# A two-layer mLSTM and windowed-attention trunk on one core: the token-wise input projection in column groups of 264, 512 and 512, and a first mLSTM chunk that starts without a barrier

## What is computed

```python
h = _rmsnorm(x, norm1_g[l])
z = h @ w_in[l]
mq, mk, mv, mi, mf, mo, aq, ak, av = jnp.split(z, split_idx, axis=-1)
qk = jax.nn.silu(_causal_dwconv(jnp.concatenate([mq, mk], axis=-1), conv_w[l], conv_b[l]))
hm = _mlstm_chunkwise(mq, mk, mv, i_pre, f_pre)          # 4 heads of 128, a recurrence over chunks
hm = _rmsnorm(hm, mlstm_norm_g[l]) * jax.nn.sigmoid(mo)
ha = _swa_sinks(aq, ak, av, sinks[l])                    # 8 query heads, 2 key heads of 64
x = x + jnp.concatenate([hm, ha], axis=-1) @ w_out[l]
h2 = _rmsnorm(x, norm2_g[l])
x = x + jnp.square(jax.nn.relu(h2 @ w_ff1[l])) @ w_ff2[l]
```

## Time and profile before

| | us |
|---|---|
| median of three runs | 2230.84 |
| the profiled execution | 2231.89 |
| its span in the trace | 2230.0 |
| PE busy | 2140.7 (96%) |
| POOL busy | 988.0 (44%) |
| DVE busy | 1424.1 (64%) |
| ACT busy | 857.6 (38%) |

### The profile page before, as it was taken

How to read it: one execution, slowest core, us unless ns; L and a number is a source line. 1 busy time by engine, 2 the same in 40 slices (tenths; PEclk the granted TensorE clock), 3 DMA queues, 4 the chain that set the end, 5 groups by cost and what they waited for, 6 DMA issues and landing times.

```text
span 2230.0 us, 34286 instructions
## 1 busy us (share of the span) xinstructions
PE 2140.7 (96%) x11748; PEld 1805.8 (81%) x11748; DVE 1424.1 (64%) x1674; ACT 857.6 (38%) x1459; POOL 988.0 (44%) x697
## 2 busy tenths in 40 slices
PE   6999998989999999999999999899899999999998
PEld 6998877878788877888899887788878887778886
DVE  4127865467777777676640488654677777876764
ACT  4224333345666642121231343432556666321210
POOL 3334524324555555445522455143245555454542
PEclk9999999999999999999999999899999999999999
DMA  7322225415777788776532223254166677987663
GB/s 261 105 92 76 72 94 179 136 70 168 255 254 241 239 304 314 306 281 256 215 129 86 90 77 111 83 174 151 39 209 237 237 237 249 348 313 292 270 273 142
DMA packets 227662, 427.29 MB, mean 192 GB/s; under 512 B 24936, under 2 KB 167016, under 8 KB 219248
## 3 DMA queue, kind: packets, MB, share of 16 engines
q1 hardware_dynamic: 212336, 402.93, 51.0%
q10 hardware_dynamic: 15232, 23.16, 2.9%
HBM read 272.79 MB, written 157.43 MB: 193 GB/s over the span
## 4 chain that ended last, share of the span: by engine, by line
PE 58%; issue 19%; POOL 12%; DVE 5%; ACT 2%; SPq 1%; DMA 1%; ACTq 1%; POOLq 0%; DVEq 0%
PE ps L1368 23%; PE ps L1714 20%; POOL w1s L1309 8%; PE ps L1553 7%; POOL w2s L1313 3%; PE ps L1666 1%; DMA uk<-uD 1%; PE ps L1472 1%; DVE y L1756 1%; DVE hT L1762 1%; PE ps L1499 1%; PE ps L1486 1%; PE ps L1591 1%; PE ps L1592 1%; PE ps L1359 1%
## 5 line engine op out<-in xcount | busy, mean ns | idle before, releaser
L1714 PE MATMUL ps<-w2s,uk 128*128 128x512 f32 x2688 | 618.6, 392 | 7.6 <-DVE uf L2249 4.1
L1714 PEld LDWEIGHTS ps<-w2s,uk 128*128 128x128 f32 x2688 | 504.8, 189 | 120.2 <-issue 11.4
L2213 DVE TENSOR_TENSOR xs<-ps,xs 128x1024 f32<-128x1024 f32 x208 | 253.4, 1222 | 171.6 <-PE ps L1714 169.9
L1666 PE MATMUL ps<-hT,w1s 128*128 128x512 f32 x1344 | 317.8, 392 | 10.6 <-DVE uf L2175 4.7
L1666 PEld LDWEIGHTS ps<-hT,w1s 128*128 128x128 f32 x1344 | 250.1, 188 | 73.4 <-issue 12.5
L1313 POOL TENSOR_TENSOR w2s<-raw,w2s 128x1024 fp32r<-128x1024 f32 x64 | 182.0, 2866 | 181.3 <-ACT w2s L1088 181.3
L1309 POOL TENSOR_TENSOR w1s<-rawf,w1s 128x512 fp32r<-128x512 f32 x112 | 170.2, 1531 | 194.3 <-ACT w1s L982 194.3
L1368 PE MATMUL ps<-hT,whi 128*128 128x512 f32 x768 | 246.3, 402 | 0.0
L1368 PE MATMUL ps<-whi,hT 128*128 128x258 f32 x1280 | 238.2, 286 | 1.0 <-DVE hT L1762 0.6
L1666 PE MATMUL ps<-tT,w1s 128*128 128x512 f32 x1008 | 237.3, 389 | 0.0
L1666 PEld LDWEIGHTS ps<-tT,w1s 128*128 128x128 f32 x1008 | 189.1, 188 | 39.5
(11 more groups left out here) (209 smaller groups left out, 3318.7 us busy)
## 6 DMA issues: line engine op xcount, KB each, us to landing
uk<-uD SPq DMA_DIRECT2D x64, 1024.0 KB, 8.7
raw<-in_wstream SPq DMA_DIRECT2D x104, 512.0 KB, 5.6
uk<-uD SPq DMA_DIRECT2D x64, 768.0 KB, 7.8
rawf<-in_wstream SPq DMA_DIRECT2D x64, 512.0 KB, 4.3
uD<-uh SPq DMA_DIRECT2D x64, 512.0 KB, 5.1
uD<-uf SPq DMA_DIRECT2D x64, 512.0 KB, 5.3
uD<-uh SPq DMA_DIRECT2D x64, 384.0 KB, 4.1
uD<-uf SPq DMA_DIRECT2D x64, 384.0 KB, 5.0
```

Of the source, the lines that this page charges most:

```text
L1666: mm = pe.matmul(ps[:, bank, :], w, x[:, k, :], start=(first and k == 0 and i == 0), stop=(k == 3 and i == 2), skip_group_check=True)
L1714: mm = pe.matmul(ps[:, bank + tp, :], u, w2s[r][:, w, k, :], start=(r in (1, 2, 5) and k == 0 and i == 0), stop=(k == 1 and i == 2), skip_ ...
L2213: V.tensor_tensor(y, ps[:, bank:bank + 2, :], y, ALU.add).then_inc(y_acc, 1)
```

## The change

Stage A has three groups of 264, 512 and 512 columns, so 24 tiles in place of 40. The arrays that the host lays out are the same, so a unit is now put together from pieces: two transfers each for units 0 to 5, three each for units 6 to 9. Group 2's split weights lie over `xs` (ACT waits for the store of x ahead of group 1). ACT splits units 2 to 5 during group 0, units 6 to 9 during group 1, and does the exponentials and squares within group 2. Group 0's result is stored by two transfers a tile.

Barrier 2 is gone (`PHASES` is 2). In the last step of stage B PE does chunk 0's scores and keys inside the last `big`, DVE's `first_chunk` weights them there, ACT and POOL split the first attention tile there. In stage C PE takes `w_out` row by row (`row`, `out_split`): rows 0 to 3 in chunk 0 and rows 4 to 7 in chunk 1, each as soon as it is split, both column halves at once. The attention half of `mxh` is multiplied with these rows first. POOL splits the `lo` of k = 3, 4 and 6, DVE of 0, 1, 2, 5 and 7. Chunk 0 doesn't multiply with the state, which is zero there.

The ring is 4 x 4 x 264 x 4 = 16896 bytes, 33 x 512, and `whi` and `wlo` are `D` words long: in the changed kernel `whi`, `wlo`, `mxh`, `mxl`, `ahi1`, `alo1`, `ahi2`, `alo2` leave 224 when divided by 512, as `hT` does.

```diff
+GC = (264, 512, 512)
+ZX = ZV + 512 - 6
...
-        raw = [ring_r(f"raw{s}", [P, 4 * GW], F32) for s in range(RING)]
+        raw = [ring_r(f"raw{s}", [P, 4 * GC[0]], F32) for s in range(RING)]
         hilo_at = ring_r.at
-        whi = [ring_r(f"whi{s}", [P, 4 * GW], F32R) for s in range(RING)]
-        wlo = [ring_r(f"wlo{s}", [P, 4 * GW], F32R) for s in range(RING)]
+
+        ahi0, alo0 = [ring_r(f"a{n}0", [P, KT, GC[0]], F32R) for n in ("hi", "lo")]
+        ahi1_at = ring_r.at
+        ahi1 = ring_r("ahi1", [P, KT, 512], F32R)
+        br = Region(hilo_at)
+        whi = [br(f"whi{s}", [P, D], F32R) for s in range(RING)]
+        br = Region(ahi1_at)
+        wlo = [br(f"wlo{s}", [P, D], F32R) for s in range(RING)]
...
                 sp.wait_ge(w_lo, l * U + max(n + 1, RING))
-                sp.dma_start(raw[slot][:], wtoken[l, n]).then_inc(s_raw[slot], 16)
+
+                def piece(g, kh, k0, ks, c0, dst):
+
+                    src = wtoken[l, 2 * g + kh].rearrange("p (k c) -> p k c", c=GW)
+                    sp.dma_start(dst, src[:, k0:k0 + ks, c0:c0 + dst.shape[2]]).then_inc(s_raw[slot], 16)
+
+                if n < 2:
+                    d = raw[slot][:].rearrange("p (k c) -> p k c", c=GC[0])
+                    piece(0, n, 0, 4, 0, d[:, :, 0:GW])
+                    piece(4, n, 0, 4, ZX - 4 * GW, d[:, :, GW:GC[0]])
+                else:
...
+                    if n < 6:
+                        piece(1, kh, k0, 2, 0, d[:, :, 0:GW])
+                        piece(2, kh, k0, 2, 0, d[:, :, GW:512])
...
-                barrier(sp, p_sp, (p_pe, p_act, p_dve, p_pool), l * PHASES + 2)
...
-                    if t in (2, 3):
-                        split_a(l, t, 0, 0)
+                    if 2 <= t < 6:
+                        if t == 2 and l > 0:
+
+                            act.wait_ge(y_m, l * YM)
+                        split_a(l, t)
...
+                act.wait_ge(n_y, (l * 2 + 1) * NT)
+                act.wait_ge(s_spill, l * (32 * NT) + 16 * NT)
+                for t in range(NT):
+                    if t < 4:
+                        split_a(l, 6 + t)
+                    evacuate(1, t)
+                for t in range(NT):
+                    evacuate(2, t)
...
-                att_hi(0, 0)
-                for k in range(4):
-                    split_out(k)
+                split_out(0); split_out(1)
                 squares(0, 0)
+                split_out(2)
                 decays(0, 1, False)
+                split_out(3)
...
+                        for k in range(KT):
+                            if last and x == 5 and k == 5:
+
+                                pe.wait_ge(b_at, (l + 1) * NT + 1)
+                                pe.wait_ge(b_pd, (l + 1) * NT + 1)
+                                scores_c(0, 0, 0, l * NT)
+                                keys_t()
...
+                    if first:
+
+                        pe.wait_ge(c_al, T + 1)
+                        pe.wait_ge(c_x, T * 2 + 2)
+                        for k in range(4):
+                            out_split(pe, l, k)
+                            for n in range(2):
+                                row(p, n, ROW[k])
...
+                def first_chunk():
+                    dve.wait_ge(c_rin[0], l * 64 + 16)
+                    V.tensor_copy(scl[:].unsqueeze(2), erB[0][:, :, P - 1:P]).then_inc(c_scl, 1)
+                    weights(0, l * NT, False)
```

More of the change, by code:

```diff
@@ L104, in trunk_kernel @@
         ta = Region(tmp_at)
-        zst = [ta(f"zst{b}", [P, GW], F32) for b in range(4)]
+        zst = [ta(f"zst{b}", [P, 512], F32) for b in range(4)]
         gN = ta("gN", [P, NT, 8], F32)
@@ L898, in _ @@
                 step_b(MH - 1, True)
-                for b in range(2):
-                    act.wait_ge(b_ao[b], (l + 1) * 64 + 1)
-                barrier(act, p_act, (p_pe, p_sp, p_dve, p_pool), l * PHASES + 2)
                 def split_out(k):
@@ L1299, in _ @@
                 plain_lo(0, 0); plain_lo(0, 1)
-                barrier(pool, p_pool, (p_pe, p_sp, p_dve, p_act), l * PHASES + 3)
-                for _ in range(4):
+                barrier(pool, p_pool, (p_pe, p_sp, p_dve, p_act), l * PHASES + 2)
+                for _ in range(5):
                     pool.sem_inc(w_lo, 1)
@@ L1423, in rows_m, with step_b @@
                     mm.then_inc(a_mn, 1)
-                group(1, 2)
-                rows_b()
-                group(2, 0)
+                for n in range(NT):
+                    tile(1, n)
+                    if n == 3:
+                        rows_b()
                 rows_t()
-                group(3, 2)
-                rows_m()
-                group(4, 0)
+                for n in range(NT):
+                    tile(2, n)
+                    if n == 3:
+                        rows_m()
                 barrier(pe, p_pe, (p_act, p_sp, p_dve, p_pool), l * PHASES + 1)
-                def step_b(j):
+                def step_b(j, last):
                     T = [l * NT + j * 2, l * NT + (j * 2 + 1)]
@@ L1445, in big @@
                         pe.wait_ge(b_ev, H + (x + 1))
-                        mm = three(ps[:, G + x % 2, :],
-                                       [(whi[s][:, k * P:(k + 1) * P], wlo[s][:, k * P:(k + 1) * P], hT[:, x % 2, 0, k, :], hT[:, x % 2, 1, k, :])
-                                        for k in range(KT)])
+                        for k in range(KT):
[4 more added lines that the diff above has]
+                                keys_t()
+                            h_, l_ = whi[s][:, k * P:(k + 1) * P], wlo[s][:, k * P:(k + 1) * P]
+                            for i, (a, b) in enumerate(((h_, 0), (h_, 1), (l_, 0))):
+                                mm = pe.matmul(ps[:, G + x % 2, :], a, hT[:, x % 2, b, k, :], start=(k == 0 and i == 0), stop=(k == KT - 1 and i == 2))
                         mm.then_inc(b_g, 1)
@@ L1529, in keys_t, with row @@
                     mm.then_inc(c_kt, 1)
-                pe.wait_ge(b_at, (l + 1) * NT + 1)
-                pe.wait_ge(b_pd, (l + 1) * NT + 1)
-                scores_c(0, 0, 0, l * NT)
-                keys_t()
-                barrier(pe, p_pe, (p_act, p_sp, p_dve, p_pool), l * PHASES + 2)
+                with pe.Fori(0, MH - 1) as j:
+                    step_b(j, False)
+                step_b(MH - 1, True)
+                def row(p, n, k):
+                    w, m = slice(n * 512, (n + 1) * 512), (k + 4) % KT
+                    for a, b in ((mxh, woh), (mxh, wol), (mxl, woh)):
+                        mm = pe.matmul(ps[:, G + n, :], a[p][:, m, :], b[:, k, w],
+                                       start=(k == 4 and a is mxh and b is woh), stop=(k == 3 and a is mxl), skip_group_check=True)
+                    return mm
                 def project(T, p, n, att_part, mix_part):
@@ L1543, in project @@
                         pe.wait_ge(c_x, T * 2 + (n + 1))
-                    for part, ks in ((att_part, range(4, KT)), (mix_part, range(0, 4))):
-                        if not part:
-                            continue
-                        if ks[0] == 0:
-                            pe.wait_ge(c_mh, T + 1)
-                            pe.wait_ge(c_ml, T + 1)
-                        for k in ks:
-                            w = slice(n * 512, (n + 1) * 512)
-                            for a, b in ((mxh, woh), (mxh, wol), (mxl, woh)):
-                                mm = pe.matmul(ps[:, G + n, :], a[p][:, k, :], b[:, k, w],
-                                               start=(k == 4 and a is mxh and b is woh), stop=(k == 3 and a is mxl))
+                        for k in range(4, KT):
+                            row(p, n, k)
                     if mix_part:
+                        pe.wait_ge(c_mh, T + 1)
+                        pe.wait_ge(c_ml, T + 1)
+                        for k in range(4):
+                            mm = row(p, n, k)
                         mm.then_inc(c_op, 1)
@@ L2042, in step_c @@
                     V.tensor_tensor(mixf[:], ps[:, TB + 1, :].rearrange("p (h c) -> p h c", c=P), gst[p][:], ALU.mult).then_inc(c_mix, 1)
-                    if not (first or second):
+                    if second:
+                        residual(l, j, p, 0, 1)
+                    if not first:
                         residual(l, j, p, 1, 1)
```

274 lines of the change are left out of this document (152 added, 122 removed).

## The result

The changed kernel is slower: 2237.97 us (median of nine runs, 2236.91 to 2241.63) against 2230.73 (nine runs of the kernel before, 2227.98 to 2234.17), ratio 1.0033 with a 95% interval of 1.0024 to 1.0042. The forecast was 2214.9, and the range of 2202 to 2229 doesn't hold the result. The profiled execution's span is 2235.3 us against 2230.0.

A forecast was written before the change was run, and what follows sets the result against it. PE, busy 2140.7 of 2230.0 us, was taken as the bound. Terms -14.2, +2, +15, -8.3 and -10.4 sum to -15.9, from 2230.84 to 2214.9 us; range 2202 to 2229.

The forecast's parts named there:

- The weights at the start: Program start: short rows of units 0 and 1 in shared queues delay PE's first stage A product, +15 us.
- R2: Rival, program start: small rows travel in groups, so the start is as early as before; 2199.9 us, chance 0.13.
- Fewer, wider matmuls: Stage A: two groups of 512 columns replace four of 258, and an ACT wait goes; -14.2 us for both layers.
- ACT stall: Last group of stage A: PE idle 1.6 us a layer while ACT does exponentials and squares, claimed to go.
- Group 0: Stage A's first group: six more columns, more DMA issues, splits and subtractions; +2 us for both layers, bounds 0 and 6.
- The distance between matmuls in B and C: Stages B and C: new start addresses of stationary operands bring matmuls 6.0 ns closer; -10.4 us, bounds 0 and -12.
- The entry of stage C: From stage B's end to stage C's even pace: the wait for wd goes, chunk 2 starts earlier; -8.3 us.
- R3: Rival, entry of stage C: gives nothing, since splits, not the barrier, were what C waited for; 2223.2 us, chance 0.09.
- R4: Rival, entry of stage C: PE's clock falls to 1.2 GHz in the first two chunks; slower, 2254.9 us, chance 0.08.

The follow-up runs named there:

- e1: Changed kernel, but the host lays out each stage A weight unit as used, one transfer of 128 rows instead of two or three; 2222.78 us, ratio 0.9969.
- e2: Changed kernel, but SP issues the 8 copies of x to the output behind unit 3, instead of ACT; 2227.43 us, ratio 0.9987.
- e7: e1 with columns in the order of the groups, so group 0's result is stored by one transfer a tile, not two; 2218.30 us, ratio 0.9932.
- e10: Changed kernel, but POOL's mask additions for chunks 0 and 1 wait until PE has transposed the last tile's probabilities; 2233.09 us, ratio 1.0010.
- e6: Changed kernel with the barrier of all five engines between stages B and C put back; 2240.26 us, ratio 1.0037.
- e3: Changed kernel, but DVE, not POOL, splits row 6 of w_out, behind hn of chunk 1; 2234.52 us, ratio 1.0009.
- e8: e3 with DVE also splitting row 4 of w_out, right behind chunk 1's keys; 2232.06 us, ratio 0.9999.
- e9: Kernel before with only addresses changed: whi, mxh, mxl at 224 or 480 past a multiple of 512, stage B's wlo at 256, 320, 352; 2230.01 us, ratio 0.9989.
- e12: e11, but DVE splits row 6 of w_out right behind the state update and ahead of hn, row 7 behind hn; 2201.21 us, ratio 0.9867.
- e11: Changed kernel with e7, e8 and e10 together; 2209.11 us, ratio 0.9896.

## Why the prediction was wrong, by its own steps

*The weights at the start*: right. +15 forecast, +15.3 measured; unit 0 at 28.2 (29.1), `gB` at 29.8 (30.4), unit 1 at 31.9 (33.3), the first product at 37.2 (37). The last link was another one, and that the number is so close is in part luck: I had PE wait for POOL's split of unit 1, which ended at 36.3; it waited for `hT`, ready at 37.2, at the end of the chain that `gB` begins. e1 and e2 gave 21.87 and 25.79 where 22 and 25.5 were forecast from turns of the two queues. R2, by which nothing would be lost there, is out: the Trainium skill's typical 9 to 17 descriptors to a packet (DMA: Bandwidth & Descriptors, Queues, rings and completion order) don't show in these counts, 139 against 138 in the stretch above.

*Fewer, wider matmuls*: -14.2 forecast, -11.1 measured. The matmuls gave what was forecast: without the gates' sums and the barrier, the wide groups of a layer take 93.5 us before and 87.7 after, 5.8 less for the 5.7 forecast. Inside them a tile's 24 starts take 5.44 us (226.7 ns each); the 229.4 of the runs of 96 comes from the first tile behind a row of small matmuls (5.55 to 5.61). The step that failed is the "ACT stall" of 1.6 us a layer. There was none: the 1.64 us in which PE was idle between 126 and 153 us are its wait at barrier 1, at the first matmul of B:

```profile
152.99 0.74 PE L1462 MATMUL ps<-ident,rq 128*128 128x128 f32 x5 [1.56 <-ACTq L354]
```

After the change this wait is 1.77 us. I read an idle share of a stretch whose end lay behind the barrier, and gave the idle time to what ACT was doing in it. A sum over a stretch needs the one row that holds the gap.

*Group 0*: +2 forecast, +5.0 measured, inside the bounds. I counted the eight DMA issues among the things "beside PE's products". In the second layer they are in a chain: copy of the result, store, store, copy of `hT`, DVE, PE. e7 shows that this was the whole of it there.

*The distance between matmuls in B and C*: -10.4 forecast; the cause was right and the size 5 ns rather than 6, which would be 8.6. Measured in B and C are 5.3. In stage B of the first layer 23 products gain 0.12 us each, 2.8 in all, and the layer's B still ends 0.2 later. The gain went into a wait that was there before, 1.43 us for `rq` and now 2.11 (and 0.61 at another step, where there was none), and one product after it ran at 1.2 GHz for part of its time, 7.3 us from first start to last end for 5.7. In the second layer the gain of 3.2 is near the forecast 3.5, because the kernel before had already lost there what the changed one loses: a wait of 2.33 us and a product of 6.7 behind it. I took PE as the bound all through B because it was 96% busy; at the last step of B the bound is DVE's chain to `rq`, and closer matmuls can only wait longer for it. e10 took the wait away, and then they were worth their price: stage B up to its last product takes 164.3 us in the first layer, 168.1 before.

*The entry of stage C*: -8.3 forecast, -1.5 measured; the largest miss, and what R3 had named. The first half was right to 0.1 us: chunk 0's `mixf` came 13.5 us after B's last matmul (forecast 13.4). The second half failed at chunk 1. I had written its chain as 9.4 us from `mixf` and a POOL split behind it. It took 10.7: DVE stood for 2.0 us while POOL split row 4. I had seen this cost (1 us a layer, bounds of 13 us in all) and estimated it away with "most of the chain's DVE steps fall between them". Here the Trainium skill's rule (SBUF — State Buffer, Who interferes with whom) would have done better than my average: DVE and GpSimd hold a common port pair for whole instructions. As the page has it, this holds for a DVE instruction with two inputs in SBUF, beside a GpSimd instruction that reads SBUF, and not for one with at most one such input outside DVE's two-port modes. So "each meeting", as I had put it, was too wide. The rows above agree with both halves: the step at 357.04 reads two SBUF operands and ends at 359.17, POOL's split at 359.15; the copy at 356.84 reads PSUM and takes its 0.16 us. And 1.6 us a layer went to the clock after the 4.18 us wait, where I had argued that the new waits would each be under 2 us. That is R4's mechanism at a tenth of its size: 1.2 GHz came for seven matmuls after a wait, not for two chunks.

*Stage D* wasn't in the sum and cost 2.8. In both layers the fifth run of 24 matmuls in D began after the same 2.06 us wait as before and took 4.62 us in place of 3.14. The change may not be the cause. Behind this wait the same 24 matmuls take 3.13 us in both layers of e6 and in one layer of e3, e7 and e8, with the code of D as it is, and 4.39 in one layer of e9, which is the kernel before at other addresses. Why the clock falls after it in one place and not in the other is open.

Of the 21 us that are missing, the entry of C has 6.8, the distance in B and C 5.1, the wide groups 3.1, group 0 3.0 and stage D 2.8. The range failed because the two largest have a common ground: what PE gains ahead of a place where it waits for another engine's chain is given back there, and behind the wait the clock can take some more. Each of my rivals touched one term and let the others stand in full.

## What to carry to other kernels

Count a transfer in a shared queue by its rows, before its bytes; if the host may lay data out, let it do so in the order and width of use. For each gain on the busiest engine, name the next place where that engine waits, and what the awaited chain is made of: an engine that comes there earlier only waits longer. A POOL instruction beside a DVE chain can cost its own length in that chain (2.0 us at 357 us), and so can a split of DVE's own that stands in the chain, so splits and masks belong where the chain isn't awaited (e10 and e12: some 12 us for two moved steps).

## What was not expected of the hardware

- The start address of a stationary operand changes the distance between matmuls of 512 columns by some 5 ns: 224 and 480 past a multiple of 512 give 5.46 to 5.48 us for 24, and 256, 288 and 352 give 5.57 to 5.61. One of two alternating operands at a slow start brings most of the loss (e9: 5.55). The two fast starts are 256 bytes apart, which suggests that period; which other starts are fast, and why, is open.
- The granted clock falls after some waits of 2 to 4 us and not after others of the same length: in e8 a wait of 3.01 us was followed by twelve matmuls in 5.49 us, one of 3.03 by twelve in 3.03. Behind a wait of 1.73 us for `rq` the product took 5.73 us in the first layers of e6 and e7, and 7.3 in the second layer of e3. What sets it besides the wait is open.
- Outside stage D, matmuls of 512 columns that took 0.6 us or more number 12 before, 30 after the change, 14 in e10, 8 in e12, but 33 in e11, which is 29 us faster than the changed kernel. This isn't a loss of the change as a whole: before it the entry of C ran other, smaller matmuls at 1.2 GHz (granted clock 0.81 and 0.73 in the earlier trace rows). Over a whole run PE is busy at 1.2 GHz for 36 us before and 33 after, 27 in e10, 33 in e11 and 14 in e12, and the mean granted clock is 0.990 before and 0.991 after.
